# Experts of a hierarchical MoE on one Trainium2 core: tokens become the stationary operand, in two 64-column halves, and float32 weights move

## The reference

```python
y = jnp.zeros((B * S, Dm), jnp.float32)
for e in range(N_EXPERTS):                       # 32
    a = jax.nn.silu(x @ w_g[e]) * (x @ w_u[e])   # 1024 -> 512, twice
    y = y + gate[:, e:e + 1] * (a @ w_d[e])      # 512 -> 1024
```

## Time and profile before

| | |
|---|---|
| median of three executions | 1146.57 us |
| lowest, highest | 1143.09, 1153.71 us |
| span of the profiled execution | 1142.0 us |
| its mean granted TensorE clock | 0.910 |
| median less that span | 4.57 us |
| TensorE matmul busy | 1083.6 us (95%) |
| TensorE weight loads busy | 882.8 us (77%) |
| VectorE, ScalarE, GpSimd busy | 402.0, 283.7, 84.8 us |
| moved by DMA | 264.56 MB |

### The profile page before, as it was taken

One profiled execution on the slowest core, in us unless ns is written; L12 is line 12 of the kernel. 1 busy time (PEld: TensorE's weight loads), 2 busy tenths in 40 slices (PEclk: granted clock), 3 DMA queues, 4 the chain that ended last, 5 costly groups with the idle time before them and its releaser, 6 DMA issues.

```text
span 1142.0 us, 16399 instructions
## 1 busy us (share of the span) xinstructions
PE 1083.6 (95%) x6668; PEld 882.8 (77%) x6668; DVE 402.0 (35%) x745; ACT 283.7 (25%) x485; POOL 84.8 (7%) x156
## 2 busy tenths in 40 slices
PE   6999999999999999989999999999999999999980
PEld 4666666456546655789999999999999999999970
DVE  1014440065312053314343525243433434252533
ACT  3013220023502133112222323131313222231321
POOL 2010000010100001400000000000000000000004
PEclk9996559965699998979999999999999999999995
DMA  8926003230204423278989899999989898988804
GB/s 238 385 96 258 1 1 111 74 120 1 74 1 161 171 74 139 91 260 321 361 340 352 337 353 340 350 354 342 370 331 365 336 357 336 355 339 324 290 11 147
DMA packets 54354, 264.56 MB, mean 232 GB/s; under 512 B 10648, under 2 KB 10672, under 8 KB 45712
## 3 DMA queue, kind: packets, MB, share of 16 engines
q1 hardware_dynamic: 46016, 236.18, 55.5%
q0 software_dynamic: 5600, 19.51, 5.5%
q10 hardware_dynamic: 2704, 8.39, 2.0%
HBM read 249.33 MB, written 16.58 MB: 233 GB/s over the span
## 4 chain that ended last, share of the span: by engine, by line
PE 91%; DVE 3%; DMA 3%; issue 1%; POOL 1%; ACT 1%; ACTq 0%; SPq 0%; POOLq 0%; DVEq 0%
PE pA L1151 39%; PE pS L1165 11%; PE pA L882 10%; PE pA L875 9%; PE pS L915 5%; PE pA L949 5%; PE pTr L1142 3%; PE pTr L930 2%; PE pA L857 2%; PE pTr L866 1%; PE pS L919 1%; DMA zone<-hn_d,idx_cur 1%; DMA zone<-y_d,slot 1%; POOL slot_d L592 1%; PE pA L1102 0%
## 5 line engine op out<-in xcount | busy, mean ns | idle before, releaser
L1151 PEld LDWEIGHTS pA<-zone,ring 128*128 128x128 f32 x4096 | 473.5, 194 | 4.6 <-issue 0.5
L1151 PE MATMUL pA<-zone,ring 128*128 128x64 f32 x4096 | 470.8, 276 | 0.0
L1487 DVE TENSOR_TENSOR zone<-zone,pS 64x1024 f32<-64x1024 f32 x32 | 38.8, 1212 | 349.2 <-ACT zone L774 349.2
L1482 DVE TENSOR_TENSOR w_lo<-ring,w_hi 128x1024 fp32r<-128x1024 f32 x128 | 150.5, 1218 | 19.8 <-ACT w_hi L761 19.8
L761 ACT ACTIVATE w_hi<-ring 128x1024 fp32r<-128x1024 f32 x128 | 127.7, 1046 | 30.5 <-DVE zone L1487 30.5
L774 ACT ACTIVATE zone<-pS 64x1024 f32<-64x1024 f32 x32 | 32.7, 1021 | 393.2 <-PE pS L1165 393.2
L882 PE MATMUL pA<-ring,hT 128*128 128x512 f32 (+1 forms) x240 | 106.3, 601 | 1.0 <-DVE hT L1236 1.0
L1165 PE MATMUL pS<-w_hi,a_split 128*128 128x512 f32 x256 | 104.1, 407 | 0.0
L1165 PE MATMUL pS<-w_lo,a_split 128*128 128x512 f32 x256 | 100.8, 394 | 0.0
L875 PE MATMUL pA<-hT,ring 128*128 128x320 f32 x320 | 91.1, 448 | 0.5 <-DVE hT L1236 0.5
L882 PEld LDWEIGHTS pA<-ring,hT 128*128 128x128 f32 (+1 forms) x240 | 41.3, 175 | 61.5 <-issue 60.9
(11 more groups left out here) (195 smaller groups left out, 732.4 us busy)
## 6 DMA issues: line engine op xcount, KB each, us to landing
ring<-in_w_exp_gate SPq DMA_DIRECT2D x32, 2048.0 KB, 10.6
ring<-in_w_exp_up SPq DMA_DIRECT2D x32, 2048.0 KB, 8.7
ring<-in_w_exp_down SPq DMA_DIRECT2D x32, 2048.0 KB, 13.9
ring<-in_w_in SPq DMA_DIRECT2D x6, 2048.0 KB, 21.4
y_d<-zone ACTq DMA_DIRECT2D x32, 256.0 KB, 5.0
ring<-in_w_out SPq DMA_DIRECT2D x2, 2048.0 KB, 18.4
ring<-in_w_ck SPq DMA_DIRECT2D x1, 2048.0 KB, 25.6
ring<-in_w_cv SPq DMA_DIRECT2D x1, 2048.0 KB, 7.7
```

What stands on the lines that cost most here:

```text
L1151: last = mm(pA[b][:, x * GW + f * SLOTS:x * GW + (f + 1) * SLOTS], w[:, c, f * P:(f + 1) * P], xeT[:, b, c, :], start=c == 0, stop=c == C - 1)
L1482: nv.tensor_tensor(w_lo[:, f, :], by_k(3 * b + 2, FC)[:, f, :], w_hi[:, f, :].bitcast(F32), ALU.subtract).then_inc(w_lo_ready, 1)
L1487: nv.tensor_tensor(ysb[:, b, :], ysb[:, b, :], pS[b][0:SLOTS, :], ALU.add).then_inc(y_summed, 1)
```

## The change

All three products now hold the tokens still and move float32 weights, 512 columns at a time. The 64 token columns fill half of the array's 128 columns, so the sum over the input is cut in two: even steps write to PSUM partitions 0 to 63, odd steps to partitions 64 to 127, and the two sums stand in the two halves of a bank. For gate and up the halves are added, and the result turned, by a further product with `fold`, two identity matrices of 64 under each other (`fold_halves`); for that ScalarE (`copy_gate`) and VectorE (`copy_up`) first copy both banks to SBUF. For down the halves are added as before by `lower_rows` and `sum_rows`. The split of the down weights and of the activations goes, and the warm-keeping matmul of the loop too. The order of an iteration becomes gate(n), up(n), down(n-1), fold(n), transposes(n+2). The wait of the load into the down buffer becomes `y_ready`, the end of the down product. The transposes use one PSUM bank in place of two.

```diff
@@ SyncE: wait before a load into a down buffer
-                    sp.wait_ge(w_lo_ready, (r * NE + e - 1) * FC)
+                    sp.wait_ge(y_ready, r * NE + e - 1)
@@ ScalarE
-            def split(b, chunks):
-                for f in chunks:
-                    act.activation(w_hi[:, f, :], by_k(3 * b + 2, FC)[:, f, :], ACT.Copy).then_inc(w_hi_ready, 1)
+            def copy_gate(n):
+                act.wait_ge(gate_read, n + 1)
+                act.activation(gusb[:, 0, :], pA[0][:, :], ACT.Copy).then_inc(gate_copied, 1)
             def sigmoid(n, b, first=False):
-                act.wait_ge(gu_ready, n + 1)
+                act.wait_ge(folded, n + 1)
...
+                copy_gate(n)
                 lower_rows(n - 1, 1 - b, first_out)
-                act.wait_ge(w_in_s[3 * b + 2], (n - b) * 8 + 48)
-                split(b, (0,))
+                sigmoid(n, b, first)
                 rows_out(n - 1, 1 - b, r, e - 1)
-                split(b, range(1, FC))
-                sigmoid(n, b, first)
@@ TensorE
             def product(n, b, x):
                 pe.wait_ge(w_in_s[3 * b + x], (n - b) * 8 + 48)
+                pe.nop().then_inc(pe_passed, 1)
                 w = by_k(3 * b + x)
-                for f in range(FC):
-                    for c in range(C):
-                        last = mm(pA[b][:, x * GW + f * SLOTS:x * GW + (f + 1) * SLOTS], w[:, c, f * P:(f + 1) * P],
-                                  xeT[:, b, c, :], start=c == 0, stop=c == C - 1)
+                for k in range(C // 2):
+                    for j in range(2):
+                        c = j * (C // 2) + k
+                        last = mm(pA[x][j * SLOTS:(j + 1) * SLOTS, :], xeT[:, b, c, :], w[:, c, :],
+                                  start=k == 0, stop=k == C // 2 - 1)
                 last.then_inc(gu_ready if x else gate_read, 1)
+            def fold_halves(n):
+                pe.wait_ge(gate_copied, n + 1)
+                pe.wait_ge(up_copied, n + 1)
+                for x in range(2):
+                    for f in range(FC):
+                        last = mm(pTr[1][:, x * GW + f * SLOTS:x * GW + (f + 1) * SLOTS], gusb[:, x, f * P:(f + 1) * P],
+                                  fold[:, :], start=True, stop=True)
+                last.then_inc(folded, 1)
             def down(n, b, first=False):
+                pe.wait_ge(w_in_s[3 * b + 2], (n - b) * 8 + 48)
                 pe.wait_ge(at_ready, n + 1)
...
-                for f in range(FC):
-                    a = a_split[:, b, f, :, :].rearrange("p k s -> p (k s)")
-                    pe.wait_ge(w_lo_ready, n * FC + f + 1)
-                    for half in range(2):
-                        for part in (w_hi, w_lo):
-                            last = mm(pS[b][0:2 * SLOTS, half * 512:(half + 1) * 512], a, part[:, f, half * 512:(half + 1) * 512],
-                                      start=f == 0 and part is w_hi, stop=f == FC - 1 and part is w_lo)
+                for half in range(2):
+                    for k in range(FC // 2):
+                        for j in range(2):
+                            f = j * (FC // 2) + k
+                            last = mm(pS[b][j * SLOTS:(j + 1) * SLOTS, half * 512:(half + 1) * 512], a[:, f, :],
+                                      w[:, f, half * 512:(half + 1) * 512], start=k == 0, stop=k == FC // 2 - 1)
@@ the iteration
-                    if not first:
-                        keep_warm(pA[b], 1, 256)
                     pe.wait_ge(xe_ready, n + 1)
                     product(n, b, 0)
+                    product(n, b, 1)
                     down(n - 1, 1 - b, first)
-                    product(n, b, 1)
+                    fold_halves(n)
                     transpose_rows(n + 2, b)
@@ VectorE
+            def copy_up(n):
+                dve.wait_ge(gu_ready, n + 1)
+                nv.tensor_copy(gusb[:, 1, :], pA[1][:, :]).then_inc(up_copied, 1)
...
             def expert(n, b, first=False):
+                copy_up(n)
                 sum_rows(n - 1, 1 - b)
-                lower_weights(n, b)
                 activations(n, b, first)
+                rows_in(n + 2, b)
```

More of the change, by code:

```diff
@@ L124, in build @@
         ysb = zone[0:SLOTS, 4096:6144].rearrange("p (b d) -> p b d", b=2)
+        gusb = zone[:, 7168:8192].rearrange("p (x f) -> p x f", x=2)
         ygat = zone[:, 0:6144].rearrange("p (t k d) -> p t k d", t=TILES, k=2)
@@ L132, in build @@
         ones = sb("ones", [P, P])
+        fold = sb("fold", [P, SLOTS])
         cmask = sb("cmask", [P, 256])
@@ L299, in build @@
         y_ready = sem("y_ready")
-        w_hi_ready = sem("w_hi_ready")
-        w_lo_ready = sem("w_lo_ready")
-        a_split_step = sem("a_split_step")
+        gate_copied = sem("gate_copied")
+        up_copied = sem("up_copied")
+        folded = sem("folded")
+        silu_step = sem("silu_step")
         y_lower = sem("y_lower")
@@ L791, in expert @@
                 n = r * NE + e
+                copy_gate(n)
                 lower_rows(n - 1, 1 - b, first_out)
-                act.wait_ge(w_in_s[3 * b + 2], (n - b) * 8 + 48)
-                split(b, (0,))
+                sigmoid(n, b, first)
                 rows_out(n - 1, 1 - b, r, e - 1)
-                split(b, range(1, FC))
-                sigmoid(n, b, first)
             def experts(r):
                 n = r * NE
-                act.wait_ge(w_in_s[2], n * 8 + 48)
-                split(0, range(FC))
                 first = isinstance(r, int)
+                copy_gate(n)
                 sigmoid(n, 0, first)
@@ L1135, in _, with transpose_rows @@
             pe.wait_ge(a_used, A_LIST + 1)
-            def transpose_rows(n, b):
+            def transpose_rows(n, b, first=False):
                 pe.wait_ge(xg_in[b], (n - b) * 8 + 16)
+                if not first:
+                    pe.wait_ge(xe_ready, n)
                 pe.nop().then_inc(pe_passed, 1)
@@ L1141, in transpose_rows @@
                 for c in range(C):
-                    last = nc.tensor.transpose(pTr[b][:, c * SLOTS:(c + 1) * SLOTS], src[:, c, :], ident[0:SLOTS, 0:SLOTS])
+                    last = nc.tensor.transpose(pTr[0][:, c * SLOTS:(c + 1) * SLOTS], src[:, c, :], ident[0:SLOTS, 0:SLOTS])
                 last.then_inc(xt_ready, 1)
@@ L1159, in down @@
                     pe.wait_ge(y_summed, n - 1)
[L1160 to L1166 removed]
+                pe.nop().then_inc(pe_passed, 1)
+                w = by_k(3 * b + 2, FC)
+                a = aT[:, b, :].rearrange("p (f s) -> p f s", f=FC)
+                for half in range(2):
[4 more added lines that the diff above has]
+                                      w[:, f, half * 512:(half + 1) * 512], start=k == 0, stop=k == FC // 2 - 1)
                 last.then_inc(y_ready, 1)
@@ L1196, in _ @@
             keep_warm(pS[0], 5)
-            transpose_rows(0, 0)
+            transpose_rows(0, 0, True)
             transpose_rows(1, 1)
@@ L1224, in _ @@
             dve.wait_ge(consts, 2)
+            nv.tensor_tensor(fold[:, :], ident[:, 0:SLOTS], ident[:, SLOTS:2 * SLOTS], ALU.add)
             nv.tensor_tensor(fla[:, 0:8], ident[:, 0:8], ident[:, 32:40], ALU.add)
@@ L1459, in rows_in @@
                 dve.wait_ge(xt_ready, n + 1)
-                nv.tensor_tensor(xeT[:, b, :, :], pTr[b][:, 0:C * SLOTS].rearrange("p (c s) -> p c s", c=C),
+                nv.tensor_tensor(xeT[:, b, :, :], pTr[0][:, 0:C * SLOTS].rearrange("p (c s) -> p c s", c=C),
                                  gcol[:, 4, :].unsqueeze(2).to_broadcast([P, C, SLOTS]), ALU.mult).then_inc(xe_ready, 1)
+            def copy_up(n):
+                dve.wait_ge(gu_ready, n + 1)
+                nv.tensor_copy(gusb[:, 1, :], pA[1][:, :]).then_inc(up_copied, 1)
             def activations(n, b, first=False):
                 dve.wait_ge(sig_ready, n + 1)
[L1466 to L1469, removed]
+                nv.tensor_tensor(sg[:, b, :], sg[:, b, :], pTr[1][:, 0:GW], ALU.mult).then_inc(silu_step, 1)
+                dve.wait_ge(silu_step, n + 1)
                 if not first:
                     dve.wait_ge(y_ready, n - 1)
[L1472 to L1482, removed]
+                nv.tensor_tensor(aT[:, b, :], sg[:, b, :], pTr[1][:, GW:2 * GW], ALU.mult).then_inc(at_ready, 1)
             def sum_rows(n, b):
@@ L1496, in experts @@
                 first = isinstance(r, int)
-                lower_weights(n, 0)
                 if first:
@@ L1500, in experts @@
                     rows_in(1, 1)
+                copy_up(n)
                 activations(n, 0, first)
+                rows_in(n + 2, 0)
                 expert(n + 1, 1, first)
```

5 lines of the change are left out of this document (1 added, 4 removed).

## The result

The changed kernel took 1056.59 us (median of four executions, 1053.75 to 1061.5) against 1150.14 us of the kernel before, run beside it (median of four, 1143.09 to 1155.6): a ratio of **0.9184**, 95% interval 0.9133 to 0.9234. The forecast was 1083 us and the range began at 1060. The direction and the mechanism held; the gain was larger than the range allowed, 88.5 us of span (1142.0 to 1053.5) in place of 64.

What follows compares the result with a forecast made beforehand. TensorE was taken as the bound, with DMA next after the change. down(0) ending at 508, 88 loads (527 us) and the end put the stage end at 1046, not 1110: span 1142 - 64 = 1078, median 1083 us; range 1060 to 1272.

Steps and rivals of the forecast that it cites:

- What bounds the kernel: Expert stage: TensorE bounds at 19.56 us an iteration, only 1.6 us above DMA's 18.0.
- Products, the two halves at once: Gate, up and down: 48 records take 10.3 us if both column halves work at once, 20.6 one after the other.
- Fold and transposes: TensorE, each iteration: fold 1.8 us, transposes 1.0; copies before the fold hidden, except 0.7 us at the first expert.
- TensorE's sum: One iteration on TensorE: 10.3 + 1.8 + 1.0 = 13.1 us with overlap, 23.4 without.
- SyncE's queue: Weight loads: three leave together at each down end; gate lands 12 us and up 18 after issue; steady state costs nothing.
- The start: First experts: TensorE idles 8 us for the gather, then two products take 13.7 at half clock; down(0) ends about 508.
- 88 loads at 6.0 us: Loads remaining after down(0): 2.28 MB each with other traffic, at 380 GB/s, 527 us in all.
- The end: End of the expert stage: last weight, down(31), lands at 1037; the stage ends at 1046 where it ended at 1110.
- the serial case: Rival in the three products: halves do not run at once, 23.4 us an iteration, 1272 us; chance 0.24.
- loads in the open: Rival in the products: 48 loads of 64 columns at 0.14 us are not hidden, iteration 19.8, 1155 us; chance 0.05.
- the clock in the gaps: Rival on TensorE: the clock falls while it idles for DMA, iteration priced at 19.2 us, 1136 us; chance 0.04.
- DMA at today's rate: Rival in the loads: DMA moves no more than 350 GB/s, 88 loads take 573 us, 1129 us; chance 0.03.

Runs made afterwards that it cites:

- the run in one half: The changed kernel with all steps of the three products writing to partitions 0 to 63, so neighbours share a column half: 1277.67 us, single execution.
- the run in blocks: The changed kernel with all steps of the lower column half first, then all of the upper, in every accumulation: 1055.93 us, single execution.
- the order of release: The changed kernel with gate and up loads of the next expert issued ahead of this one's down load: 1045.76 us (0.9079), again 1049.28 us (0.9118).
- the down load of an eighth: The changed kernel with the down load of experts 2 to 31 cut to 256 KB, TensorE's work unchanged: 947.27 us, single execution.

## Why the prediction was wrong where it was

- **What bounds the kernel**: right. TensorE stood just above DMA, and the lead of TensorE was all there was to gain in a steady iteration. It was 2.5 us (19.56 less 17.03) and not 1.6.
- **Products, the two halves at once**: right, 10.45 us against 10.3, and shown by the run in one half. My reason for the in-between order (starts keep the program's order) was wrong, as the run in blocks shows; it did not enter the sum. The rule of the Trainium skill ("TensorE: Matmul & The Clock Gate", Part 3) that column tiles run side by side holds here for float32, at 2.0 times (0.218 against 0.435 a record). The prediction took nearly the full factor from it. Its figure, 2.38 for three tiles, is 0.79 of the full factor; as an estimate that would give two halves 1.6 and the three products 13 us, and the run measured 10.45. Its sentence in "The mechanism" that a weight load overlaps only where the row group differs does not hold here: loads of 64 columns in one row group are hidden in steps of 0.43. The same section also lets a load go ahead into a background weight buffer, and that fits. Its other rule there, matmuls strictly in program order at their start, does not fit the starts at 513.35 and 513.77 either.
- **Fold and transposes**: 1.93 and 1.02 against 1.8 and 1.0. Copies hidden, as said; the first one showed 0.9 us where 0.7 was put.
- **TensorE's sum**: 13.4 against the 13.1 forecast.
- **SyncE's queue**: right in that an idle DMA shows at the start, which the order of release took away for the most part, and none in the loop. The landings were mis-sized: gate 19.6 and up 25.8 us after the issue (medians of the page) where I had 12 and 18, since loads of the iteration before were still under way.
- **The start**: mis-sized. I had down(0) end at 508; it ended at 501.6, 6.4 us sooner. The wait for the gather came (6.9 us), and a half clock behind it, but that lasted some 3 us: the granted clock was 0.53 from 489.66 to 492.80 and 1.00 from there. The two products took 8.5 us and not 13.7, the down product 3.6 and not 5. I had carried over the 13.9 us at 0.50 of the kernel before. There the wait was shorter (3.2 us) and other matmuls followed it; no run parts the two, so why the clock came back sooner is open.

```profile
488.61 1.12 PE L1138 MATMUL pTr<-ident,zone 64*128 64x64 f32 x8 [6.92 <-DMA zone<-hn_d,idx_cur]
489.66 8.52 PE L1149 MATMUL pA<-ring,zone 128*64 128x512 f32 x32
498.01 3.60 PE L1176 MATMUL pS<-ring,zone 128*64 128x512 f32 x16
```

- **88 loads at 6.0 us**: the step that failed. "I take 380" stood between rows of 372, 387 and 397. DMA moved 397 GB/s over 475 us. From the issue at 501.66 to the landing of up(31), which TensorE sees at 1003.94, 87 loads took 502.3 us with the last one's latency, 5.77 each; I had 523. That is 21 us. The rows could not carry the number: windows of 10 us scatter widely at full share. In the changed kernel, whose long mean is 397, they go from 351 to 440 GB/s, and in the kernel before a window of 10 us inside the first of the earlier trace rows, which has 387 over 20 us, has 424 (the first line here; the other two are of the changed kernel):

```profile
35.00:45.00 10.00, 10.00 (x39) 7.07 (x38) 0.00 (x0) 0.87 (x2) 0.00 (x0) 1.00 1.12 424
```

```profile
750.00:760.00 10.00, 10.00 (x58) 5.47 (x56) 3.35 (x5) 1.40 (x2) 1.10 (x2) 1.00 1.04 440
760.00:770.00 10.00, 8.35 (x40) 2.99 (x36) 0.69 (x1) 0.60 (x1) 0.00 (x0) 1.00 1.01 351
```

  The number of loads under way does not sort the three rows: by the issues and landings in the trace it was two or three in the window with 387, two but for 0.3 us in the one with 372, and only one for 3.2 of the 10 us in the one with 397. Nor does the depth of the queue explain the gain over 380, as two under way have 394. Whether the kernel before could have held 397, or only 380, is open.
- **The end**: from that landing to the end of the stage 18 us against 15; 1.7 of the 3 are the last up product, which ran partly at half clock (5.35 us in place of 3.65).

Together 6.4 + 21 - 3 = 24.4 of the 24.5 us between the span I forecast and the span of the profile. The range of the likeliest case allowed 395 GB/s (1063 us), but alone, with the start as forecast. Each of the two errors by itself would have stayed in the range; both point the same way, and together they fall below 1060. The rivals: the serial case is excluded; loads in the open, excluded; **the clock in the gaps** does happen (5.35 us for a product of 3.65, mean clock 0.95), but as said then, TensorE catches up, and the run in blocks at full clock is no faster. DMA at today's rate, excluded.

## What to carry to other kernels

Float32 matmuls with 64 rows of output need not leave half of the array idle: two accumulations over halves of the input, in the two column halves, in turn, run at the price of one; a fold afterwards costs little. When TensorE stands a little above DMA, the gain is what lies between them, so take the DMA rate from as long a stretch as there is, let the range hold its scatter and that of the start together, count loads and not iterations, and look for the loads that can leave before the stage. A TensorE row that looks worse may cost nothing where another resource is the bound: read it in a window in which that resource does not hold it up.

## What the runs showed of the hardware

- Float32 matmuls with 512 moving columns and 64 columns of output take 0.218 us a record when neighbours lie in different column halves, 0.435 when all lie in one, and 0.257 (12.34 us for 48) in blocks of one half after the other.
- Column halves do not keep one order of starts: the half that is ahead starts records that stand later in the program (513.35 before 513.77).
- The clock after a wait. In the changed kernel 32 records of 512 columns took 8.5 us after a wait of 6.9 us, and 9.6 in a second trace after 5.1, where they take 7.1 at full clock. In the kernel before, 64 records of 64 columns took 13.9 us after a wait of 3.2 us, with the granted clock at 0.50 to their end, where they take 7.3 at full clock.
- The clock can fall without a wait: in the run in one half it was 0.93 from 707 to 730 us, with TensorE busy without a gap.
- One weight load of 2048 KB at a time moves 276 GB/s, two at a time 394, two to five at a time 398 (all from 540 to 980 us).
- DMA's share can stand at 1.00 while it moves 370 GB/s and TensorE is the bound (the down load of an eighth).
